# Prompt weights of layer 1's attention split in SBUF and turned by transposing DMAs

## What is computed

```
def mla_block(q_lat, q_rope, qpos, ckv, krope, kpos):
    s = (einsum('bqhc,bkc->bhqk', q_lat, ckv) + einsum('bqhr,bkr->bhqk', q_rope, krope)) * (NOPE + ROPE_DIM) ** -0.5
    mask = (kpos[None, :] // CHUNK) <= (qpos[:, None] // CHUNK)
    p = softmax(where(mask, s, NEG_INF))
    return einsum('bhqk,bkc->bqhc', p, ckv)
o = einsum('bthc,chd->bthd', o_lat, w_uv)
```

## Time and profile before

| | |
|---|---|
| median of 3 runs | 2212.67 us (2211.76 to 2214.09) |
| the profiled execution | 2193.22 us, its span 2191.5 us |
| PE busy over the span | 1773.4 us (81%) |
| DVE, ACT, POOL busy | 1318.3 us (60%), 958.8 us (44%), 211.0 us (10%) |
| mean granted TensorE clock | 0.909 |

### The profile page before, as it was taken

How to read it: one execution, slowest core, us unless ns; L and a number is a source line. 1 busy time by engine, 2 the same in 40 slices (tenths; PEclk the granted TensorE clock), 3 DMA queues, 4 the chain that set the end, 5 groups by cost and what they waited for, 6 DMA issues and landing times. The chain is left out here.

```text
span 2191.5 us, 34271 instructions
## 1 busy us (share of the span) xinstructions
PE 1773.4 (81%) x12686; PEld 1351.7 (62%) x12757; DVE 1318.3 (60%) x2843; ACT 958.8 (44%) x1893; POOL 211.0 (10%) x320
## 2 busy tenths in 40 slices
PE   5859348999998984899989956798857788888787
PEld 1228235788876773677766744586755666666576
DVE  1055355788899963788885434421766566666654
ACT  1241135322811273778862153387225555655311
POOL 0000010000000102111000000100014112120000
PEclk9979669999999996999998977899988999999799
DMA  7712250443223318998734422321452100100532
GB/s 251 280 60 81 49 110 1 117 125 105 82 65 95 106 44 196 223 226 215 205 105 157 135 106 61 92 69 48 105 118 45 36 25 24 31 25 17 156 113 96
DMA packets 235198, 229.96 MB, mean 105 GB/s; under 512 B 147829, under 2 KB 171653, under 8 KB 235016
## 3 DMA queue, kind: packets, MB, share of 16 engines
q1 hardware_dynamic: 225562, 198.41, 34.2%
q0 software_dynamic: 9472, 29.36, 3.6%
HBM read 173.48 MB, written 54.23 MB: 104 GB/s over the span
## 5 line engine op out<-in xcount | busy, mean ns | idle before, releaser
L352 PE MATMUL PS<-ab_wh,hT 128*128 128x512 f32 x576 | 229.2, 398 | 10.4 <-DVE ab_wl L545 10.0
L354 PE MATMUL PS<-ab_wh,hT 128*128 128x512 f32 x576 | 225.4, 391 | 0.0
L353 PE MATMUL PS<-ab_wl,hT 128*128 128x512 f32 x576 | 225.0, 391 | 0.0
L958 DVE TENSOR_SCALAR_CACHE_REDUCE topk_junk<-scores,topk_small 128x528 bf16<-128x528 f32 (+6 forms) x224 | 194.6, 915 | 1.3
L2022 DVE CUSTOM_DVE_ANT_0 la_S<-PS,la_mask 128x128 f32<-128x128 f32 (+3 forms) x144 | 107.6, 747 | 46.6 <-PE PS L354 33.9
L352 PEld LDWEIGHTS PS<-ab_wh,hT 128*128 128x128 f32 x576 | 108.7, 189 | 33.5 <-ACT ab_wh L477 6.9
L352 PE MATMUL PS<-out_wh,out_mT 128*128 128x512 f32 x288 | 121.0, 420 | 9.8 <-DVE out_wl L1517 9.4
L1304 ACT ACTIVATE at_P<-at_S,at_nm 128x128 f32<-128x128 f32 (+2 forms) x144 | 110.4, 767 | 37.3 <-DVE at_nm L1349 37.2
L354 PEld LDWEIGHTS PS<-ab_wh,hT 128*128 128x128 f32 x576 | 108.5, 188 | 23.4
L353 PEld LDWEIGHTS PS<-ab_wl,hT 128*128 128x128 f32 x576 | 108.9, 189 | 21.5
L353 PE MATMUL PS<-out_wl,out_mT 128*128 128x512 f32 x288 | 117.5, 408 | 0.0
(11 more groups left out here) (408 smaller groups left out, 4579.0 us busy)
## 6 DMA issues: line engine op xcount, KB each, us to landing
ada_w_tiles<-in_ada_w SPq DMA_DIRECT2D x32, 768.0 KB, 5.6
ab_w<-in_ab_w_in SPq DMA_DIRECT2D x64, 256.0 KB, 2.9
out_g<-scratch_gates_nat SPq DMA_DIRECT2D x18, 512.0 KB, 6.0
at_kc<-in_cache_a_k SPq DMA_DIRECT2D x8, 1024.0 KB, 16.3
at_vc<-in_cache_a_v SPq DMA_DIRECT2D x8, 1024.0 KB, 10.4
at_kc<-in_cache_b_k SPq DMA_DIRECT2D x8, 1024.0 KB, 9.5
at_vc<-in_cache_b_v SPq DMA_DIRECT2D x8, 1024.0 KB, 5.2
scratch_qcT<-q_T SPq DMA_DIRECT2D x72, 96.0 KB, 2.0
```

The lines of the kernel that those rows point to most:

```text
L352: nc.tensor.matmul(out, x[0], w[0], start=start, stop=False)
L353: nc.tensor.matmul(out, x[0], w[1], start=False, stop=False)
L354: return nc.tensor.matmul(out, x[1], w[0], start=False, stop=stop)
L958: go(V.tensor_scalar(mark, x, limit, 0.0, op, ALU.add, accum_out=cnt[:, m:m + 1]), 0 if m == M - 1 else 1)
```

## The change

For head steps the weights are no longer turned on PE. ACT casts `Psb` (SBUF) to bfloat16, the high half. POOL (even steps) or DVE (odd steps) subtracts it from `Psb` and writes the low half beside it into `Pb`. SP issues one transposing DMA for both halves, from `Pb` to `PT` with 2(i+1) blocks of 128 x 128 bfloat16. PE multiplies with the values three steps later instead of one. `Pb` has three slots, `PT` four. The staging tile `xs` has two slots instead of three. Batch steps are still turned on PE, but unscaled; their value product has its operands exchanged, ACT scales the result by the inverse sum while it leaves PSUM (`nat`), and PE turns it back (a new unit "back"). SP's queue has the first two batch loads ahead of the steps and the others in the list of transposes. The two weight tables `u` have a semaphore each. The core of the diff:

```
-    FIRST, END = -2, N + 1
+    LAG, SLOTS = 3, 4
+    FIRST, END = -2, N + LAG
+    lowers = lambda hs: (hs + 1) // 2 if hs % 2 else hs // 2 + 1
...
-        PT, PTs = sb("PT", [P, 2, 2, QT, P], BF16), sb("PTs", [P, 2, nk + 1, P])
+        Pb, PT, PTs = sb("Pb", [P, 3, 2 * SEQ], BF16), sb("PT", [P, SLOTS, 2 * QT, P], BF16), sb("PTs", [P, 2, nk + 1, P])
...
+            load_batch(0)
             load_head(1)
-            for g in range(2, HC + 2):
-                if g % 2 == 0 and g // 2 - 1 < NB:
-                    load_batch(g // 2 - 1)
-                if g < HC:
-                    load_head(g)
+            load_batch(1)
+            for it in range(N):
+                kind, g, i = order[it]
+                if kind == "head":
+                    hs, n = QT * g + i, (i + 1) * P
+                    if hs >= SLOTS:
+                        sp.wait_ge(valued, hs - SLOTS + 1)
+                    sp.wait_ge(lowered[hs % 2], lowers(hs))
+                    sp.dma_start(PT[:, hs % SLOTS, 0:2 * (i + 1), :], Pb[:, hs % 3, 0:2 * n], transpose=True).then_inc(PT_in[hs % SLOTS], 16)
+                    if i == 0 and g and g + 1 < HC:
+                        load_head(g + 1)
+                    if i == 6 and g % 2 == 1 and (g + 3) // 2 < NB:
+                        load_batch((g + 3) // 2)
...
+            def lower(s):
+                kind, g, i = order[s]
+                hs, n = QT * g + i, (i + 1) * P
+                if kind == "head" and hs % 2 == 0:
+                    pool.wait_ge(cast, hs + 1)
+                    pool.wait_ge(expanded, n_op[0])
+                    nc.gpsimd.tensor_tensor(Pb[:, hs % 3, n:2 * n], Psb[:, s % 2, 0:n], Pb[:, hs % 3, 0:n], ALU.subtract).then_inc(lowered[0], 1)
...
+            for it in range(FIRST, END):
+                for job in early[it]:
+                    if job in wide_at:
+                        split(wide_at[job], *job, sum(1 for s in range(it) if order[s][0] == "head" and (QT * order[s][1] + order[s][2]) % 2 == 0))
+                if 0 <= it < N:
+                    lower(it)
...
             def value_head(s, g, i):
-                for j in range(len(parts(s))):
-                    wait_unit_done(pe, number["turn", s, j])
+                hs = QT * g + i
+                pe.wait_ge(PT_in[hs % SLOTS], 16 * (hs // SLOTS + 1))
...
-                    nc.tensor.matmul(PS[:, bank(m), 0:P], lat[:, b % 2, j, :], PTs[:, l % 2, j, :], start=j == 0, stop=False)
+                    nc.tensor.matmul(PS[:, bank(m), 0:P], PTs[:, l % 2, j, :], lat[:, b % 2, j, :], start=j == 0, stop=False)
...
-            pe.wait_ge(u_in, 32)
+            def turn_back(s):
+                m = number["back", s, 0]
+                wait_unit_done(pe, number["value", s, 0])
+                wait_unit_free(pe, m)
+                nc.tensor.transpose(PS[:, bank(m), 0:P], nat[:, order[s][1] % 2, :], c.ident[:]).then_inc(turned, 1)
...
             for x in range(2):
-                act.wait_ge(u_in, 32)
+                act.wait_ge(u_in[x], 16)
...
-                    if s >= 2:
-                        act.wait_ge(turned, number["turn", s - 2, len(parts(s - 2)) - 1] + 1)
+                    if s >= 2 and order[s - 2][0] == "batch":
+                        act.wait_ge(turned, number["turn", s - 2, 1] + 1)
+                    elif s >= 2:
+                        before = QT * order[s - 2][1] + order[s - 2][2]
+                        act.wait_ge(lowered[before % 2], lowers(before))
...
+                    if kind == "head":
+                        hs = QT * g + i
+                        act.wait_ge(exped, s + 1)
+                        if hs >= 3:
+                            act.wait_ge(PT_in[(hs - 3) % SLOTS], 16 * ((hs - 3) // SLOTS + 1))
+                        nc.scalar.activation(Pb[:, hs % 3, 0:widths(s)], Psb[:, s % 2, 0:widths(s)], ACT.Copy).then_inc(cast, 1)
...
-                    nc.vector.tensor_scalar(Psb[:, it % 2, 0:KEYS], Psb[:, it % 2, 0:KEYS], ri[:, l:l + 1], None, ALU.mult).then_inc(normed, 1)
...
+                    if kind == "head" and hs % 2 == 1:
+                        n = (i + 1) * P
+                        dve.wait_ge(cast, hs + 1)
+                        nc.vector.tensor_tensor(Pb[:, hs % 3, n:2 * n], Psb[:, it % 2, 0:n], Pb[:, hs % 3, 0:n], ALU.subtract).then_inc(lowered[1], 1)
```

More of the change, by code:

```diff
@@ L1600, in parts @@
     def parts(s):
[L1601 to L1604, removed]
-    FIRST, END = -2, N + 1
+        return [(0, nk, P), (nk, 1, TS)]
+    LAG, SLOTS = 3, 4
+    FIRST, END = -2, N + LAG
+    lowers = lambda hs: (hs + 1) // 2 if hs % 2 else hs // 2 + 1
+    step_of = {QT * g + i: place["head", g, i] for g in range(HC) for i in range(QT)}
     early = {it: [] for it in range(FIRST, END)}
@@ L1620, in latent_attention @@
         early[batch_at(2 * b) - 5].append(("kr", b, 0))
-    late = {batch_at(HC - 1) + 2 + n // 2: [("o", m, 0) for m in (n, n + 1)] for n in (0, 2)}
+    late = {batch_at(HC - 1) + 3 + n // 2: [("o", m, 0) for m in (n, n + 1)] for n in (0, 2)}
     seq = []
@@ L1624, in latent_attention @@
         seq += early[it]
-        if 0 <= it < N:
+        if 0 <= it < N and order[it][0] == "batch":
             seq += [("turn", it, j) for j in range(len(parts(it)))]
+        if 0 <= it - 2 < N and order[it - 2][0] == "batch":
+            seq.append(("back", it - 2, 0))
         if 0 <= it - 1 < N and order[it - 1][0] == "batch":
@@ L1735, in _, with split @@
             pool.wait_ge(mask_done, 2)
-            for e, (kind, a, half) in enumerate(wide):
+            def lower(s):
[5 more added lines that the diff above has]
+                    nc.gpsimd.tensor_tensor(Pb[:, hs % 3, n:2 * n], Psb[:, s % 2, 0:n], Pb[:, hs % 3, 0:n], ALU.subtract).then_inc(lowered[0], 1)
+            def split(e, kind, a, half, ahead):
+                if ahead:
+                    pool.wait_ge(lowered[0], ahead)
                 wait_unit_done(pool, number[kind, a, half])
@@ L1744, in _ @@
                             rows = slice(NOPE * h, NOPE * (h + 1))
[L1745 removed]
+                            expand(k[rows, a % 2, h, d, cols], xs[rows, e % 2], k[rows, a % 2, h, 0, cols] if d else None)
                 else:
@@ L1793, in unit @@
                 if kind == "o":
-                    wait_unit_done(pe, number["value", batch_at(HC - 2 if a < 2 else HC - 1), 0])
+                    wait_unit_done(pe, number["back", batch_at(HC - 2 if a < 2 else HC - 1), 0])
                     for m in range(2):
@@ L1837, in turn_weights @@
             def turn_weights(s):
[L1838 to L1842, removed]
+                pe.wait_ge(exped, s + 1)
                 for j, (first, n, w) in enumerate(parts(s)):
@@ L1885, in _ @@
                         score_batch(s, g)
-                if 0 <= it < N:
+                if 0 <= it < N and order[it][0] == "batch":
                     turn_weights(it)
-                if 0 <= it - 1 < N:
-                    kind, g, i = order[it - 1]
-                    if kind == "head":
-                        value_head(it - 1, g, i)
-                    else:
-                        value_batch(it - 1, g)
+                if 0 <= it - 2 < N and order[it - 2][0] == "batch":
+                    turn_back(it - 2)
+                if 0 <= it - LAG < N and order[it - LAG][0] == "head":
+                    value_head(it - LAG, *order[it - LAG][1:])
+                if 0 <= it - 1 < N and order[it - 1][0] == "batch":
+                    value_batch(it - 1, order[it - 1][1])
                 for job in late.get(it, []):
@@ L1951, in _ @@
                         src = PS[0:w, bank(m), 0:n * P]
-                        if kind == "head":
-                            act.wait_ge(turned, m + 1)
-                            nc.scalar.activation(PT[:, hs % 2, 0, first:first + n, :].rearrange("p a b -> p (a b)"), src, ACT.Copy).then_inc(high, 1)
-                        elif j == 1:
+                        if j == 1:
                             act.wait_ge(turned, m + 1)
```

76 lines of the change are left out of this document (39 added, 37 removed).

## The result

| | before | after |
|---|---|---|
| median of 4 runs each, same chip | 2212.22 us | 2275.34 us (2262.11 to 2281.74) |
| ratio | | 1.0279, 95% interval 1.0232 to 1.0327 |
| span of the profiled execution | 2191.5 us | 2274.7 us |

The change makes the kernel 2.8% slower, 63 us. The forecast was 2185 us and faster. The sign was wrong, and 2275 lies inside the range only because other cases were counted in.

What follows compares the result with a forecast made beforehand. PE was taken as the bound, with every second head lengthened by its wait for krope. Seven pairs -22.2, first pair -3.3, start -2.9, end +0.3 sum to -28.1, from median 2212.7 to 2185 us; range 2155 to 2300.

Steps and rivals of the forecast that it cites:

- The batch loads: PE's wait for a batch's krope load, with slow clock and refilling, costs 9.0 us seven times, 63 us, and goes away.
- PE at 14.0 us a head, not the bound by its sum: PE's work per head at full clock falls from 17.96 to 14.0 us without the head transposes, so PE stops bounding.
- PE has 4 us of slack a head: PE's spare time in each head, said to hide a slow clock after a stall of 3 us.
- ACT's own work, 14.0: ACT's casts, exponentials and evictions without its waits, 14.0 us a head.
- Splits ahead of subtractions, 8.1 a pair: POOL's splits of new keys and values delay its subtractions, and so ACT, by 8.1 us a pair of heads.
- Contention of DVE and POOL: Both subtracting from SBUF hold each other up: between none and 1.9 us, taken as 1.0 a pair of heads.
- The landing, 2.0 + 0.275(i+1): Time in us for step i's transposing DMA to land, at 240 GB/s, estimated from loads into SBUF.
- one of the signs of being wrong: In SP's queue, issuing a transpose in over 2 us would show the forecast wrong.
- The rivals of a slow queue: Transposing DMAs in the queue: at 150 GB/s 2223 us (chance 0.22); or the queue itself as bound (chance 0.22).
- D: The prediction's landing time of a transposing DMA, 2.0 + 0.275(i+1) us, taken from loads into SBUF.
- Start and end: Start of the stage 2.9 us shorter as each weight table has its own semaphore; end of the stage 0.3 longer.
- The walk: ACT followed step by step through a head from the end of cast 5: 17.8 us, 14.0 work and 3.8 waits.

Runs made afterwards that it cites:

- run 1: The kernel before with only the batch loads issued over a head ahead, weights still turned on PE: 2154.9 us, ratio 0.9779.
- run 2: The changed kernel with POOL's subtraction put ahead of its splits of new keys and values in each iteration: 2191.7 us, ratio 0.9949.
- Run 3: The changed kernel with all subtractions on DVE, none on POOL: 2183.9 us, ratio 0.9895.
- run 4: The changed kernel with a plain DMA copy of the same bytes, not turned, for each transposing DMA: 2237.0 us, ratio 1.0133.
- run 10: The changed kernel with all subtractions on DVE ahead of mask and maximum, and a plain copy for the transposing DMA: 2136.3 us, ratio 0.9723.
- runs 5 and 6: DVE's subtraction moved ahead of mask and maximum of two steps later, on run 2 (2173.3 us) and on Run 3 (2171.5 us).
- run 11: run 9 with PE multiplying the values four steps behind instead of three: 2142.2 us, ratio 0.9740.
- run 9: The changed kernel with all subtractions on DVE ahead of mask and maximum, and four slots of Pb instead of three: 2163.6 us, ratio 0.9832.
- runs 12 and 14: Head and batch loads issued behind steps 2 and 4 instead of 0 and 6, on run 9 (2152.2 us) and on run 11 (2132.4 us).
- run 14: run 11 with head and batch loads issued behind steps 2 and 4 instead of 0 and 6: 2132.4 us, ratio 0.9666.
- run 13: The changed kernel in its own order, with four slots of Pb and PE's value four steps behind: 2200.2 us, ratio 0.9994.

## Why the prediction failed

The sum expected a stage 28 us shorter and it came out 65 longer (405.0 us before and 470.3 after, from SP's issue of the first u table to the start of the last copy into `mix`). Point by point:

- **The batch loads,** 9.0 a pair: run 1 has 7.1. Too high by 1.9 x 7 = 13 us as a price of the loads, but no term of the sum: the walk replaced the whole pair.
- **PE at 14.0 us a head, not the bound by its sum:** in the piece from 1700 to 2000 PE is busy 196.7 us in some 10.9 heads, 18.0 a head. The clock is 0.78 in the mean, and the prediction's 14.0 was at full clock. "PE has 4 us of slack a head" did not hold once PE stood for landings (97.9 us) and came back at a lower clock. Of that clock's own share no run tells: it is higher in most runs where PE is busier, and none changed it alone.
- **ACT's own work, 14.0:** 27.5 a head less 12.7 of waits is 14.8. Near.
- **Splits ahead of subtractions, 8.1 a pair:** 9.0 by run 2 against after, place right too (42.1 us of waits before the batch exponential, 31.5 before step 0). But the sum had it in seven pairs, 57 us, and run 2 is 16 x 4.5 = 72 us of stage under after: 15 too few.
- **Contention of DVE and POOL:** 1.0 a pair, bounds 0 to 1.9. The 1024-wide subtraction took 1572 ns against 1245. Run 3 is under run 2 by 0.5 points, 12 us or 1.5 a pair, and by the copies only by 0.4 a pair. Inside the bounds either way. The Trainium skill, SBUF — State Buffer, Who interferes with whom, says that a DVE instruction with two SBUF inputs contends with a GpSimd (here POOL) instruction that reads SBUF; the trace agrees in kind (0.33 us in the mean, 0.91 for the 768 wide one of run 2).
- **The landing, 2.0 + 0.275(i+1):** right up to step 6 (3.7 for the step 5 shown, 3.65 expected). Step 7's takes 5.0 in the middle against 4.2, with 2.7 of issue by SP, which is one of the signs of being wrong that the prediction had listed. The rivals of a slow queue did not happen: 1568 packets for a step 5, at about 215 GB/s while they fly. So the sign came out by none of the rivals priced. The Trainium skill's 350 to 400 GB/s (Advanced Engine Details and Errata, X-Bar Transpose) are not seen here. In the middle SP's issue takes 0.86 us longer than a copy's, and D holds it by luck: it came from loads of HBM, 3.0 us for 256 KB, where run 4's copy inside SBUF lands in 2.5. A copy would be 32 us better (run 4) or 33 (run 10), so the part of the landing that the transposing adds is on the path.
- **Start and end.** From SP's first issue to ACT's first xs it took 1661.56 - 1650.45 = 11.1 us, before 1647.98 - 1633.42 = 14.6: 3.4 less, 2.9 expected. The end took 8.6 us, 7.1 before: 1.5 more, 0.3 expected.
- **The walk: 17.8 us a head, "14.0 of work and 3.8 of waits".** This is the step that failed. Run 2, which has no split in the way, takes 23.0. The 5.2 us too few are 16 x 5.2 = 83 us; the sum had 7 of them as contention, so 76 of the 90 us between 2185 and 2275 are the walk's, and the splits' 15 are the rest.

ACT's waits in run 2 say where the 5.2 lie. For DVE's subtraction it waits 3.3 a head (53.0 over 16), where the walk had 0.65; for landings 4.4 (69.8), where it had 3.15; for PE and POOL 0.45, where it had nothing; and its own work is 14.8 and not 14.0.

What the walk left out: it followed ACT alone, with DVE, the landing and, but for its splits, POOL answering at once, and took every score and maximum to be there. DVE and PE have an order too. DVE's subtraction stood behind a maximum that waited for PE (1.3 a head by runs 5 and 6); PE's scores of the step three ahead stood behind a value that waited for a landing, and the exponentials came late by it (1.0 a head by run 11 over run 9, once run 9's slot, another 1.0, had taken ACT's own wait away); the loads stood between DMA 6 and 7 (0.3 to 0.7 by runs 12 and 14). Together these runs give back 3.6 to 4.0 a head, but not all of that is part of the 5.2: the fourth slot also takes away waits for landings that the walk had. POOL in the loop is 0.2 by run 3, less than the 0.5 a head that was priced apart for contention. What is left in run 14 (19.1 a head) is mostly ACT's wait for the maximum, 45.8 us or 2.9 a head. DVE, which takes the maximum, waits 27.2 us for PE's scores and 17.7 for ACT's casts, and it is busy 80% of the time, PE 78%. Whether PE's clock, PE's order or DVE's own load makes this rest was not tried.

So the cause is shown in its parts: the loads gave 49 us, the splits ahead of POOL's subtractions cost 73, and what is left, 63 + 49 - 73 = 39, is the closed loop through DVE's order, the landing and PE's value, net of the transposes that PE no longer does. The split into parts depends on the order in which they are taken out (1.5 points are shared, run 13), and the clock's share in each is open. The transposing DMAs as such were no mistake: with the order and the slack right they beat PE's transposes, 19.1 us a head against 20.5.

## What to carry to other kernels

A walk over one engine gives a lower bound of a loop, not its time: write down for each engine in the loop what stands in front of the instruction that releases the next, and whether that one waits. When work goes from an engine to a DMA, the path gets a landing longer, 3.4 us here; give it slots and lag enough in every place where someone stands for it, for opening one of two gives little (9 us for the fourth slot, 20 more with the lag). And short urgent operations go ahead of long ones that nobody waits for: two lines moved in POOL's program were worth 73 us.

## What the runs showed of the hardware

- A transposing DMA from SBUF to SBUF occupies SP for 1.18 us at least and 1.33 in the middle; it grows with the size, to 2.7 in the middle and 3.5 at most for 512 KB (after). A plain one of the same bytes takes 0.46 in the middle and 0.60 at most (run 4).
- It moves in small packets, 1568 for 0.39 MB, some 250 bytes each, and the core's 16 DMA engines are 0.83 busy in run 14's stage at 162 GB/s, where plain copies (run 10) have 0.48 busy at 164 GB/s. Landings of the transposing DMAs were 3.4 to 3.7 us in the middle in every run, those of the plain copies 2.6 to 2.7.
- A DVE subtraction of 128x1024 from SBUF takes 1.25 us in the mean where POOL only splits (run 3), 1.57 in after and 2.05 in the head shown, with POOL splitting beside it; one of 128x768 takes 0.97 in run 3 and 1.88 in run 2.
